# Delta rule on 32-column blocks, a rotation without products, and Strassen slots for the even layer's queries and keys

## The chip, the cores and the metric

The kernel runs on one core of one Trainium2 chip. All arithmetic is in 32-bit floats. The metric is the device time of one execution in microseconds (us), the median of several runs. The engines are named as in the profile: PE is TensorE (PEld its weight loads), DVE is VectorE, ACT is ScalarE, POOL is GpSimd, SP issues the DMAs. Each engine takes its instructions in the order in which they are written for it, and waits on semaphores that the others count up.

## The reference

Two networks of two layers each run one after the other on 512 latent tokens (and, in the first network, 256 context tokens) of width 1024. The change lies in the first layer of the first network, the "even" one. It projects the normed input to queries, keys and values of a differential attention (4 heads, each with two maps of 64 channels), and of a gated delta rule (4 heads of 128 channels, in both directions). What matters here:

```python
def apply_rope(x, cos, sin):
    xf = x.astype(f32).reshape(*x.shape[:-1], x.shape[-1] // 2, 2)
    x0, x1 = xf[..., 0], xf[..., 1]
    out = jnp.stack([x0 * cos - x1 * sin, x0 * sin + x1 * cos], axis=-1)
...
    decay = jnp.exp(jnp.where(causal, g[..., :, None] - g[..., None, :], -jnp.inf))
    kk = jnp.einsum('bhncd,bhnsd->bhncs', k, k)
    lmat = jnp.where(strict, beta[..., :, None] * decay * kk, 0.0)
    rhs = jnp.concatenate([beta[..., None] * v, (beta * jnp.exp(g))[..., None] * k], axis=-1)
    sol = lax.linalg.triangular_solve(jnp.eye(GDN_CHUNK, dtype=f32) + lmat, rhs,
                                      left_side=True, lower=True, unit_diagonal=True)
...
    def step(s, inp):
        u = u0_c - w_c @ s
        o = qg_c @ s + aqk_c @ u
        s = gl_c[..., None, None] * s + jnp.swapaxes(kg_c, -1, -2) @ u
```

## The kernel before, in words

Activations lie with channels on the 128 partitions and tokens along the row: T = 768 tokens (512 latent, 256 context), NT = 6 tiles of 128 tokens. KD = 8 blocks of 128 make up the width of 1024. Weights come through a ring of two buffers, WC[0] and WC[1], 256 output columns each (a slot). SP fills a buffer again when a semaphore says that its products are done. Every engine has one hand-written program; nothing plans the order at run time.

**The slots of even_qk.** Queries and keys of the differential attention are 1024 columns, four slots of two 128-column tiles. The first slot's tiles are begun by `first_tiles` (L1094) while the normed input appears. The other three slots are six plain products by `cols_phase` (L770): eight steps of 512 and 256 tokens each. `copies` on ACT (even tiles) and DVE (odd tiles) brings them to `F`. Each 32-bit product stands in the trace as two records, with a weight load each. Behind it come the gates (L1131) and the values (L1121). Other stages of the kernel (up0 is the first) already use slots by Strassen's scheme: DVE makes sums of weight blocks (`block_sums`) and of input blocks (`input_differences`, `input_sums`), PE makes seven products of half size instead of eight (L970), ACT copies two of them out of PSUM and DVE combines all seven (`combine`). Semaphores: u_ws and u_bs for the sums, u_m for the products, u_copy, u_free and u_out for the copies and combinations.

**The differential heads.** For each of four heads, queries and keys are scaled (L2917, d_norm), a product with the matrix rotA swaps neighbours of each pair of channels (L1222), and DVE multiplies by the tables sinA and cosA and adds (L2923 to L2925). Between these PE makes later column tiles of the layer (L770) and modulation rows (L1058); then scores, softmax, transposes and the product with the values follow. POOL meanwhile makes the short convolution of the delta heads before, four channel blocks a round (L3454 to L3462).

**The delta heads.** Each head has 12 matrices of 128 by 128, 6 tiles in 2 directions d. The unit triangular matrix (from gL, made of the key products psc and the gate gB) is inverted by doubling: level e joins blocks of width 2^e. The inverse Y stands in gY, its transpose X in gX. Level 0 is a masked copy of gL over an identity (L3006) and a transpose (L3009). For e = 1 to 5 PE makes L times Y in three groups of four tiles (`products`, L1361), ACT copies them to gS (L2146), PE multiplies by X (`updates`, L1377), and DVE copies the entries of the level under a mask into gY (L3029) and transposes (L3023). These products are 64x64, two a tile. The last level joins the two halves of 64 (`last_products` L1388, `last_updates` L1400). Then W is made (L1437), and a scan over the six tiles runs both directions step by step (L1451 to L1464), with DVE keeping the state.

In the gaps of the levels stands work for the next head n: on PE its sums of squares (`delta_sums`) and of decays (`delta_decay`), both L1195, on POOL its squares (L3494) and decay rows (L3503), on ACT its silus, logarithms and exponentials, on DVE `gates_of`, `differences`, `beta_gate` and `normalise`. The output of the head before (`head_out`) is also made there.

Of the kernel before, what the change touches and what calls it, by code (L numbers as in the profile page):

```python
# [17 lines left out]
P = 128  # L18
D = 1024
KD = D // P  # L20
LAT, CTX = 512, 256
# [16 lines left out]
R_CY, R_X, R_Y = 3 * (LAST - 1) + 2, 2 + 3 * (LAST - 2) + 2, 2 + 3 * (LAST - 1)  # L38
QUARTER = [(slice(0, 32), slice(32, 64)), (slice(96, 128), slice(64, 96))]
CORNER = [(slice(64, 128), slice(0, 64)), (slice(0, 64), slice(64, 128))]  # L40
QUARTERS = (slice(0, 64), slice(64, 128))
# [16 lines left out]
def shape_constants():  # L58
# [6 lines left out]

    r = np.zeros((P, P))
    e = np.arange(0, P, 2)
    r[e + 1, e] = -1.0
    r[e, e + 1] = 1.0
    c["rotA"] = r  # L70
# [14 lines left out]
    idx = (p % 64) // 2  # L85
    c["cosA"] = np.cos(ang)[:, idx].T
    c["sinA"] = np.sin(ang)[:, idx].T
    lev = []
    for b in range(LAST):
        w = 1 << b  # L90
        same = p[:, None] // (2 * w) == p[None, :] // (2 * w)
        low = same & (p[:, None] // w % 2 == 1) & (p[None, :] // w % 2 == 0)
        lev.append(np.stack([low.T, low], 1))
    c["levels"] = np.stack(lev, 1).reshape(P, LAST * 2 * P)
# [8 lines left out]
def offsets(parts):  # L103
    at, out = 0, {}
    for name, width in parts:
# [5 lines left out]
CONST_PARTS = [("ident", P), ("ones", P), ("sel32", 34), ("half", P), ("rotA", P), ("upto", 2 * P),  # L111
               ("near", GRID), ("dil", 2 * P), ("cosA", LAT), ("sinA", LAT),
               ("levels", LAST * 2 * P), ("invp", 1)]
# [16 lines left out]
LINEAR = [("even_qk", 2, 4), ("even_v", 1, 3), ("even_b", 4, 8),  # L130
# [10 lines left out]
STAGES = [("up0", 22), ("down0", (4, 4, 3)), ("up1", 22), ("down1", (4, 4, 3)), ("sc_in", 12), ("mup0", 16),  # L141
# [27 lines left out]
def views(nc, ctx):  # L169
# [11 lines left out]
    extra = sb("extra", 3 * P)  # L181
    psl = ctx.enter_context(nc.psum_tensor("ps_lin", [P, 2, 1024], F32))
# [20 lines left out]
    m["levels"] = cut(const, CONST_AT["levels"][0], LAST, 2, P).bitcast(mybir.dt.uint32)  # L203
# [37 lines left out]
    m["gL"], m["gX"], m["gY"] = (cut(h, i * 1536, 12, P) for i in range(3))  # L241
    m["gq"], m["gk"], m["gv"] = ([m["FB"][:, 4 * i, :]] + [cut(t, i * T, T) for t in (big, x, big)] for i in range(3))
# [31 lines left out]
    m["STR"] = {"up0": (up_sums, up_weights, up_parts),  # L274
# [117 lines left out]
def network(nc, a):  # L392
    with ExitStack() as ctx:
# [40 lines left out]
        def _(sp):  # L434
# [312 lines left out]
        def _(pe):  # L747
# [360 lines left out]
            cols_phase("even_qk", 2, T, begun_tiles=2)  # L1108
# [201 lines left out]
            def delta_head(h):  # L1310
# [30 lines left out]
                if h:  # L1341
                    pe.wait_ge(s.r_oln, h)
# [2307 lines left out]
```

## Time and profile before

| what | value |
|---|---|
| median of 3 runs | 3975.91 us |
| lowest, highest | 3975.55, 3978.28 us |
| profiled execution, its own time | 3969.4 us |
| span of its profile | 3966.6 us |
| PE busy | 3847.7 us, 97% |
| DVE, ACT, POOL busy | 55%, 21%, 18% |
| mean granted PE clock | 0.996 |

Start times in the rows count from the span's start. A row of the timeline merges neighbouring instructions of one line: its length reaches from the first start to the last end, "x" is their count, and the brackets hold idle time ahead of it and what ended it. Since a matmul's end lies behind the start of the next one, the spacing of starts tells more than the lengths.

### The profile page before, as it was taken

How to read it: one execution, taken by the hardware profiler on the slowest of the kernel's cores; microseconds unless marked ns; L12 is line 12 of the kernel's file. 1: busy time of each engine (PE TensorE's matmuls, PEld its weight loads, DVE VectorE, ACT ScalarE, POOL GpSimd, SP SyncE). 2: the span in 40 equal slices, each digit the busy share in tenths (PEclk: the TensorE clock that was granted, in tenths of full speed). 3: DMA queues.
4: the chain of work that ended last, by engine and by line, in shares of the span. 5: the costliest groups of instructions: out<-in, count | busy, mean ns of one | idle time of the engine just before them, and what ended most of it. 6: DMA issues, size and time to landing. Idle time of an engine off the chain costs nothing.

```text
span 3966.6 us, 48576 instructions
## 1 busy us (share of the span) xinstructions
PE 3847.7 (97%) x18642; PEld 2876.9 (73%) x18642; DVE 2168.3 (55%) x3779; ACT 824.2 (21%) x1463; POOL 712.9 (18%) x570
## 2 busy tenths in 40 slices
PE   7999978999999999999999999999999999999998
PEld 3445567565555555688888877888789898778886
DVE  2144476354446312326555665664788888556546
ACT  2144565221010014632110101000311111110002
POOL 0038853100000000000000001120144343121200
PEclk9999999999999999999999999999999999999999
DMA  5244300131211121112322322232222222122321
GB/s 182 85 162 167 117 23 2 65 96 53 63 53 59 58 74 33 42 53 76 85 85 94 83 79 85 85 107 90 77 70 69 63 74 69 53 85 85 101 85 64
DMA packets 381407, 312.19 MB, mean 79 GB/s; under 512 B 9552, under 2 KB 349904, under 8 KB 381136
## 3 DMA queue, kind: packets, MB, share of 16 engines
q1 hardware_dynamic: 381264, 310.23, 25.2%
q8 instruction: 97, 1.59, 0.2%
q14 instruction: 46, 0.38, 0.0%
HBM read 308.10 MB, written 2.10 MB: 78 GB/s over the span
## 4 chain that ended last, share of the span: by engine, by line
PE 92%; DVE 3%; ACT 3%; issue 1%; DMA 1%; SPq 0%; DVEq 0%; ACTq 0%
PE ps_lin L970 18%; PE ps_lin L870 10%; PE ps_d L970 9%; PE ps_lin L770 7%; PE ps_lin L1706 6%; PE ps_d L870 5%; PE ps_c L970 4%; PE ps_lin L753 4%; PE ps_lin L816 3%; PE ps_d L753 3%; PE ps_lin L1121 3%; PE ps_c L870 3%; PE ps_d L1495 2%; PE ps_c L753 2%; PE ps_d L1706 1%; PE ps_d L1058 1%
## 5 line engine op out<-in xcount | busy, mean ns | idle before, releaser
L3430 POOL TENSOR_TENSOR rstd<-square 128x512 f32<-128x512 f32 (+2 forms) x12 | 15.1, 1258 | 1556.1 <-ACT square L1893 1556.1
L970 PE MATMUL ps_lin<-arena,ring 128*128 128x256 f32 (+1 forms) x800 | 217.2, 424 | 1.1 <-DVE arena L2572 1.1
L870 PE MATMUL ps_lin<-arena,ring 128*128 128x256 f32 (+1 forms) x864 | 214.1, 401 | 0.0
L970 PEld LDWEIGHTS ps_lin<-arena,ring 128*128 128x128 f32 x800 | 151.9, 190 | 60.8 <-issue 2.9
L870 PEld LDWEIGHTS ps_lin<-arena,ring 128*128 128x128 f32 x864 | 164.2, 190 | 41.0
L970 PE MATMUL ps_lin<-hid_in,arena 128*128 128x256 f32 x832 | 188.6, 380 | 3.6 <-DVE arena L2599 3.6
L770 PE MATMUL ps_lin<-hid_in,ring 128*128 128x512 f32 (+1 forms) x576 | 189.3, 486 | 1.1 <-DMA ring<-in_even_w_in 1.1
L3433 POOL TENSOR_TENSOR rstd<-rstd,square 128x512 f32<-128x512 f32 (+2 forms) x58 | 75.2, 1297 | 630.6 <-ACT square L1893 629.6
L970 PE MATMUL ps_lin<-hid_in,mixed 128*128 128x384 f32 (+1 forms) x672 | 187.8, 433 | 0.0
L970 PE MATMUL ps_d<-arena,mixed 128*128 128x384 f32 (+1 forms) x672 | 187.8, 433 | 0.0
L2596 DVE TENSOR_TENSOR arena<-ring 128x1024 f32<-128x1024 f32 x84 | 103.1, 1227 | 147.6 <-PE ps_d L870 135.6
L970 PEld LDWEIGHTS ps_lin<-hid_in,arena 128*128 128x128 f32 x832 | 157.7, 190 | 27.6 <-DVE arena L2599 5.6
L770 PEld LDWEIGHTS ps_lin<-hid_in,ring 128*128 128x128 f32 x576 | 109.2, 190 | 79.4 <-issue 70.7
L970 PEld LDWEIGHTS ps_d<-arena,mixed 128*128 128x128 f32 x672 | 127.7, 190 | 53.1
L970 PEld LDWEIGHTS ps_lin<-hid_in,mixed 128*128 128x128 f32 x672 | 127.7, 190 | 53.1
L970 PE MATMUL ps_lin<-hid_in,ring 128*128 128x256 f32 x704 | 159.7, 380 | 3.4 <-issue 1.7
L970 PEld LDWEIGHTS ps_lin<-hid_in,ring 128*128 128x128 f32 x704 | 133.5, 190 | 23.7 <-issue 3.3
L2207 ACT ACTIVATE arena<-ps_lin 128x256 f32<-128x256 f32 (+1 forms) x96 | 39.0, 406 | 520.7 <-PE ps_lin L970 513.0
L2596 DVE TENSOR_TENSOR mixed<-ring 128x1024 f32<-128x1024 f32 (+1 forms) x66 | 80.6, 1222 | 116.1 <-PE ps_d L870 101.1
L1893 ACT ACTIVATE square<-resid 128x512 f32<-128x512 f32 (+2 forms) x104 | 63.2, 612 | 359.0 <-DVE resid L2746 99.3
L3569 POOL TENSOR_TENSOR arena<-ring 128x1024 f32<-128x1024 f32 x32 | 77.1, 2411 | 297.3 <-PE ps_d L1706 201.2
L1877 ACT ACTIVATE arena<-ps_lin 128x256 f32<-128x256 f32 (+1 forms) x32 | 13.1, 410 | 563.2 <-PE ps_lin L870 563.2
(545 smaller groups left out, 8100.1 us busy)
## 6 DMA issues: line engine op xcount, KB each, us to landing
ring<-in_ffn_w_in SPq DMA_DIRECT2D x88, 512.0 KB, 5.0
resid<-in_ada_w SPq DMA_DIRECT2D x20, 2048.0 KB, 8.1
ring<-in_mlp_w_up SPq DMA_DIRECT2D x64, 512.0 KB, 4.3
ring<-in_mlp_w_down SPq DMA_DIRECT2D x64, 512.0 KB, 4.4
ring<-in_attn_w_qkv SPq DMA_DIRECT2D x64, 512.0 KB, 4.5
ring<-in_ffn_w_out SPq DMA_DIRECT2D x32, 512.0 KB, 4.4
ring<-in_even_w_in SPq DMA_DIRECT2D x28, 512.0 KB, 5.1
ring<-in_sc_w_in SPq DMA_DIRECT2D x24, 512.0 KB, 4.6
```

Of the source, the lines that this page charges most:

```text
L753: last = mm(out, lhs, rhs, start=(j == 0), stop=(j == len(pairs) - 1))
L770: last = mm(psl[:, par, u:v], lhs, rhs[:, u:v], start=(j == 0), stop=(j == len(pairs) - 1))
L816: last = mm(psl[:, n, at:at + v - u], w[:, k, n * P:(n + 1) * P], O[:, k, u:v], start=(k == 0), stop=(k == KD - 1))
L870: last = mm(prod[i - 1], lhs[:, j, :], rhs(p), start=(g == j == 0), stop=(g == G - 1 and j == np_ - 1))
L970: last = mm(out, lhs[:, j, :], rhs[:, j, :], start=(j == 0), stop=(j == 3))
L1121: last = mm(psl[:, t % 2, 0:width], H[:, k, t * P:(t + 1) * P], weights[:, k, :], start=(k == 0), stop=(k == KD - 1))
L1495: last = mm(psd[:, u:v], WC[h % 2][:, k, P:2 * P], H[:, k, u:v], start=(k == 0), stop=(k == KD - 1))
L1706: last = mm(out, lhs[:, j, :], rhs[:, j, :], start=(j == 0), stop=(j == 3))
L1893: fn(SQ[:, k % 2, u:v], X[:, k, u:v], ACT.Square).then_inc(s.n_sq, 1)
L2596: tt(ws["sum"][:, 0:np_, :], r1, r2, add)
L3433: tt(acc, acc, m["SQ"][:, k % 2, c0:c1], ALU.add).then_inc(s.n_acc, 1)
L3569: tt(ws["sum"], r1, r2, ALU.add)
```

## The change

Three things change together.

1. **Levels up to the fifth keep 32-column blocks.** New tiles cX, cY and cS hold, for each of the 12 matrices, only the four diagonal blocks of 32 by 32, that is 128 partitions by 32 columns. `turned_blocks` brings gL in this form by products with an identity; levels e = 0 to 4 are masked copies and transposes of 6 tiles by 32 columns for each direction, and `products` and `updates` make four 32x32 products a tile, in two groups (one a direction) instead of three. Level 5, the pair step, joins neighbouring blocks of 32: `pair_products` and `pair_updates`. ACT and DVE then place the diagonal blocks and the pairs in gY and gX for the last level, which stays. gX and gY are cleared once by DVE; POOL sets the identity in cY for the next head.
2. **Work for the next head is re-ordered.** Its squares move from POOL to ACT. Its first sum stands behind the pair step, its second sum and its two decay sums between the steps of the scan; the logarithms, exponentials, `beta_gate`, `differences` and `normalise` move there as well. The transposes of the keys go to psc. A head's key products now wait for r_diff and r_qe of both directions.
3. **Rotation and even slots.** The host orders the query and key channels of each map so that the first parts of the pairs are 32 neighbours and the second parts the next 32. DVE then rotates by reading the other 32 partitions, without a product. The last three slots of even_qk use Strassen's scheme, with products in the order 3, 4, 5, 2, 1, 7, 6.

The core of the diff:

```diff
-LINEAR = [("even_qk", 2, 4), ("even_v", 1, 3), ("even_b", 4, 8),
+LINEAR = [("even_qk", 2, 1), ("even_v", 1, 3), ("even_b", 4, 8),
...
-            for sl in range(2):
-                sp.wait_ge(buf_full[1], BUFS["even_qk"] + sl + 1)
-                fill_cols(ew, sl, 512 + sl * 256)
+            sp.wait_ge(buf_full[1], BUFS["even_qk"] + 1)
+            fill_cols(ew, 0, 512)
+            sp.wait_ge(s.u_m, 3)
+            fill_cols(ew, 1, 768)
...
-                half_done("even_qk")(sl)
+                sp.wait_ge(s.u_m, 7 * (sl + 1) + 3)
...
             pe.wait_ge(s.wg_in, 16)
+            pe.wait_ge(s.u_out, 6)
...
-                for j, (q, ps) in enumerate([("QN", psc[:, 0:LAT]), ("KN", psc[:, LAT:2 * LAT])]):
-                    pe.wait_ge(s.d_norm, 2 * h + j + 1)
-                    mm(ps, m["rotA"], m[q][:, 0:LAT], start=True, stop=True).then_inc(s.d_rot, 1)
+                pe.wait_ge(s.d_rs, 2 * h + 2)
...
                 pe.wait_ge(s.r_norm, 2 * h + 2)
+                pe.wait_ge(s.r_diff, 2 * h + 2)
+                pe.wait_ge(s.r_qe, 2 * h + 2)
...
+                def products(e, d):
+                    c = 2 * (e - 1) + d
+                    pe.wait_ge(s.r_y, R_Y * h + c + 1)
+                    if e == 1:
+                        pe.wait_ge(s.r_vt_out, h + 1)
+                    for t in range(NT):
+                        j = d * NT + t
+                        for r in QUARTERS:
+                            last = mm(CYB[d][r, t * 32:(t + 1) * 32], gL[r, j, r], cY[r, j, :], start=True, stop=True)
+                    last.then_inc(s.r_cy, 1)
+
+                def updates(e, d):
+                    c = 2 * (e - 1) + d
+                    pe.wait_ge(s.r_cy_out, R_CY * h + c + 1)
+                    pe.wait_ge(s.r_x, R_X * h + c + 1)
+                    for t in range(NT):
+                        j = d * NT + t
+                        for r in QUARTERS:
+                            last = mm(YCYB[d][r, t * 32:(t + 1) * 32], cX[r, j, :], cS[r, j, :], start=True, stop=True)
+                    last.then_inc(s.r_ycy, 1)
...
+                pair_products()
+                pair_updates()
+                if n is not None:
+                    pe.wait_ge(s.r_kq_out, 2 * h + 2)
+                    if h == 0:
+                        pe.wait_ge(s.mod_new, H_EVEN)
+                    delta_sums(n, 0, SIDE)
...
+                    if i == 0:
+                        pe.wait_ge(s.r_ln, 2 * n + 1)
+                        delta_sums(n, 1, SIDE)
+                    if i == 2:
+                        pe.wait_ge(s.r_ln, 2 * n + 2)
+                        delta_decay(n, 0, SIDE)
+                    if i == 4:
+                        pe.wait_ge(s.r_qe, 2 * n + 1)
+                        delta_decay(n, 1, SIDE)
```

On ACT and DVE of a delta head (heads of the levels and of the scan):

```diff
+                for e in range(1, PAIR):
+                    for d in range(2):
+                        act.wait_ge(s.r_cy, R_CY * h + 2 * (e - 1) + d + 1)
+                        fn(half(cS, d), blocks(CYB[d]), ACT.Copy).then_inc(s.r_cy_out, 1)
+                    if e == 1 and h:
+                        out_rstd(h - 1)
+                    if n is not None and e > 1:
+                        silu(n, e - 2)
+                        if e < 4:
+                            head_square(n, e - 2)
...
+                if n is not None:
+                    gate_of(h)
+                    logs()
+                    log_of(n, 0, SIDE)
+                else:
+                    gate_of(h)
...
+                    if i == 1:
+                        log_of(n, 1, SIDE)
+                        exp_gate(n)
+                    if i == 2:
+                        rstd_of_head(n)
+                    if i == 3:
+                        exp_rows(n, 0, SIDE)
+                        exp_decay(n, 0)
+                if n is not None:
+                    exp_rows(n, 1, SIDE)
+                    exp_decay(n, 1)
...
+                for e in range(PAIR):
+                    for d in range(2):
+                        dve.wait_ge(s.r_eye, 2 * h + 4)
+                        dve.wait_ge(s.r_ycy, R_YCY * h + 2 * e + d + 1)
+                        dve.copy_predicated(half(cY, d), over_tiles(m["levels"][:, e, d, :]), blocks(YCYB[d]))\
+                            .then_inc(s.r_y, 1)
+                        dve.wait_ge(s.r_y, R_Y * h + 2 * e + d + 1)
+                        dve.transpose(half(cX, d), half(cY, d)).then_inc(s.r_x, 1)
+                    if e == 0 and n is not None:
+                        gates_of(n)
+                    if e == 1:
+                        query_key(0)
+                        query_key(1)
...
+                    if e == 2 and h:
+                        head_out(h - 1, 0)
+                    if e == 3 and h:
+                        head_out(h - 1, 1)
...
+                    if i == 2:
+                        beta_gate(n)
+                        differences(n, 0, SIDE)
+                    if i == 3:
+                        normalise(n, 0)
+                    if i == 4:
+                        normalise(n, 1)
+                if n is not None:
+                    differences(n, 1, SIDE)
```

Here PAIR is 5, QUARTERS are the four slices of 32 partitions, h is the head and n the next one (none for the last).

## Rows read from the trace of the kernel before

**Rows 1.** The page: busy us of PE (share of span, instructions); chain that ended last

```profile
PE 3847.7 (97%) x18642; PEld 2876.9 (73%) x18642; DVE 2168.3 (55%) x3779; ACT 824.2 (21%) x1463; POOL 712.9 (18%) x570
...
PE 92%; DVE 3%; ACT 3%; issue 1%; DMA 1%; SPq 0%; DVEq 0%; ACTq 0%
```

**Rows 2.** Timeline, PE, rest of even_qk: start us, us, engine, line, operation

```profile
61.47 62.08 PE L770 MATMUL ps_lin<-hid_in,ring 128*128 128x512 f32 x192
```

**Rows 3.** Timeline, PE, two neighbouring Strassen slots of the up0 stage

```profile
858.19 5.32 PE L970 MATMUL ps_lin<-arena,ring 128*128 128x384 f32 x16
...
876.25 5.32 PE L970 MATMUL ps_lin<-arena,ring 128*128 128x384 f32 x16
```

**Rows 4.** Timeline, DVE: last operation before even_qk; four input sums of up0

```profile
53.63 0.22 DVE L2827 TENSOR_REDUCE small<-arena 128x1 f32<-128x64 f32 x1
...
828.36 1.96 DVE L2554 TENSOR_TENSOR arena<-hid_in 128x384 f32<-128x384 f32 x4
```

**Rows 5.** Timeline, PE: the rotation of the first differential head

```profile
187.10 1.98 PE L1222 MATMUL ps_c<-mixed,const 128*128 128x512 f32 x4
...
188.92 10.48 PE L770 MATMUL ps_lin<-hid_in,ring 128*128 128x512 f32 x32
```

**Rows 6.** Timeline, POOL: start of the last round of convolutions

```profile
419.29 1.44 POOL L3439 COPY mixed<-arena 128x768 f32 x1 [2.87 <-DVE mixed L2917]
```

**Rows 7.** Timeline, PE: delta heads, from the first to the stage behind them

```profile
498.31 1.60 PE L1321 MATMUL ps_c<-arena 128*128 128x128 f32 x12
...
559.68 1.50 PE L1321 MATMUL ps_c<-arena 128*128 128x128 f32 x12
...
566.35 0.68 PE L1361 MATMUL ps_lin<-hid_in 64*64 64x64 f32 x16
...
575.02 1.56 PE L1195 MATMUL ps_d<-square,const 128*128 128x512 f32 x4
...
594.77 1.61 PE L1377 MATMUL ps_lin<-arena,hid_in 64*64 64x64 f32 x32 [1.72 <-issue]
...
597.67 2.16 PE L1195 MATMUL ps_d<-resid,const 128*128 128x512 f32 x4
...
599.76 1.43 PE L1388 MATMUL ps_lin<-hid_in 64*64 64x64 f32 x24
...
605.57 0.39 PE L1451 MATMUL ps_c<-arena,hid_in 128*128 128x128 f32 x2
...
682.54 1.50 PE L1321 MATMUL ps_c<-arena 128*128 128x128 f32 x12
...
732.99 2.82 PE L794 MATMUL ps_lin<-mixed,ring 128*128 128x512 f32 x8 [1.19 <-DVE arena L3071]
```

**Rows 8.** Timeline, ACT and DVE: single operations of the second delta head

```profile
561.72 1.28 ACT L1829 ACT_TABLE_LOAD   x1
...
563.01 0.81 ACT L2132 ACTIVATE arena<-ps_lin 128x768 f32<-128x768 f32 x1
...
568.97 0.60 ACT L2146 ACTIVATE arena<-ps_lin 128x512 f32<-128x512 f32 x1 [0.25 <-PE ps_lin L1361]
...
562.28 1.03 DVE L3006 COPY_PREDICATED hid_in<-const,hid_in 128x768 f32<-128x768 uint32 x1
...
571.03 0.73 DVE L3029 COPY_PREDICATED hid_in<-const,ps_lin 128x512 f32<-128x512 uint32 x1 [0.26 <-PE ps_lin L1377]
...
537.71 0.77 DVE L3042 STREAM_TRANSPOSE hid_in<-hid_in 32x192 f32<-32x192 f32 x2
```

**Rows 9.** Timeline, PE: four small products (eight records) with 32 weight columns

```profile
511.98 0.28 PE L1065 MATMUL ps_d<-mixed,const 128*32 128x40 f32 x8
```

**Rows 10.** Groups, PE, 0 to 745 us, shapes apart: count, busy us, mean ns

```profile
L1065 PE MATMUL ps_d<-mixed,const 128*32 128x40 f32 x32 | 1.1, 216 | 0.0
```

**Rows 11.** Windows: busy us of PE, PEld, DVE, ACT, POOL; granted clock

```profile
592.00:594.00 2.00, 0.68 (x16) 0.57 (x16) 1.98 (x2) 1.31 (x3) 2.00 (x2) 1.00 0.00 0
...
596.00:598.00 2.00, 1.77 (x25) 1.49 (x22) 1.38 (x3) 0.00 (x0) 1.23 (x1) 0.50 0.04 8
```

More of the change, by code:

```diff
@@ new lines, in delta_head @@
+                for d in range(2):
+                    turned_blocks(d)
+                for t in range(NT):
+                    last = pe.transpose(psc[:, t * P:(t + 1) * P], gk[:, t * P:(t + 1) * P], ident)
+                last.then_inc(s.r_kt, 1)
+                for e in range(1, PAIR):
+                    for d in range(2):
+                        products(e, d)
+                    if e == 1:
+                        if h:
+                            pe.wait_ge(s.r_oln, h)
+                        for t in range(NT):
+                            c = slice(t * P, (t + 1) * P)
+                            last = mm(psd[:, c], gk[:, c], gq[:, c], start=True, stop=True)
+                        last.then_inc(s.r_kq, 1)
+                    for d in range(2):
+                        updates(e, d)
+                    if e == 2 and h == 0:
+                        mod_slot(H_EVEN - 1, MOD_STEPS)
@@ L1817, in _ @@
             chain = Chain(act, s.act_step)
-            def copies(name, iters, dst, width):
-                b = BUFS[name]
-                with act.Fori(0, iters) as i:
-                    for sl in range(2):
-                        act.wait_ge(buf_full[0], b + 2 * i + sl + 1)
-                        fn(flat(dst)[:, ds((4 * i + 2 * sl) * width, width)], psl[:, 0, 0:width], ACT.Copy)\
-                            .then_inc(buf_free[0], 1)
             def logs():
@@ L1933, in _ @@
             shifts("mix0", T)
-            copies("even_qk", 2, m["F"], T)
+            act.wait_ge(buf_full[0], BUFS["even_qk"] + 1)
+            fn(m["F"][:, 0, :], psl[:, 0, 0:T], ACT.Copy).then_inc(buf_free[0], 1)
+            for u in range(3):
+                if u:
+                    act.wait_ge(s.u_free, 3 * u - 1)
+                for i in range(2):
+                    act.wait_ge(s.u_m, made(u, 3 + i))
+                    fn(m["STR"]["even_qk"][2][i], m["PROD"][2 + i][:, 0:T // 2], ACT.Copy).then_inc(s.u_copy, 1)
             act.wait_ge(s.g_raw, 1)
@@ new lines, in delta_head @@
+                for q in QUARTERS[1:]:
+                    diagonal(q)
+                act.wait_ge(s.r_ycy, R_YCY * (h + 1) - 2)
+                for d in range(2):
+                    pair(d, 0)
+                for d in range(2):
+                    lo, up = CORNER[d]
+                    act.wait_ge(s.r_cy, R_CY * (h + 1) - 1 + d)
+                    fn(half(gS, d)[up, :, lo], corners(CYB[1][up, :]), ACT.Copy).then_inc(s.r_cy_out, 1)
+                act.wait_ge(s.r_x, R_X * (h + 1))
+                for d in range(2):
+                    pair(d, 1)
```

426 lines of the change are left out of this document (196 added, 230 removed).

## Prediction

> **What bounds the kernel now.** I read the page first: PE is busy 97% of the span and carries 92% of the chain that ended last [rows 1]. So time is won only where PE has less to do or waits less. The timeline of PE then shows three stretches that the change touches. The rest of even_qk is one unbroken block of 62.08 us [rows 2]. The four differential heads are dense too; in each the rotation takes PE from 187.10 to 188.92 [rows 5]. The delta heads are the only long stretch with idle between PE's groups: the first takes 61.37 us, the two after it 61.43 each, the last, up to the 1.19 us of waiting ahead of even_out, 49.26 [rows 7]. There a level is a circle of PE product, ACT copy, PE product, DVE masked copy, so it is bound by latencies and by the order in the queues of ACT and DVE. Five levels of a middle head, with four sums for the next head among them (1.5 us each), last from 566.35 to 599.76, which is 33.4 us [rows 7].
>
> **Part 1: even slots.** Six plain products go; three Strassen slots come. Two such slots of the same width start 18.06 us apart [rows 3], so PE needs 3 x 18.06 = 54.2 us for the 62.0 us that the block takes up to the next stage. DVE must first make the sums. It is free at 53.85 [rows 4]. Four sums of 384 columns take 1.96 us, the next starts 0.47 behind the last [rows 4]: 20 input sums make 9.4 us, and the weight sums, 2560 columns in four operations, 3.0. DVE ends at 66.3, then it copies tile 1 (0.9 us), which frees the bank for the third product at 67.2. PE is there at 61.47 + 5.16 = 66.6, so it waits 0.6. At the end PE must wait for DVE's last combination, a 384-column addition of 0.5 us and two hand-overs: 0.85. Sum: 54.2 + 0.6 + 0.85 - 62.0 = **-6.3 us**. On SP the fills of the last two slots and of the values wait for counts of Strassen products, each at least four products (10 us) ahead of its use; that cover hides their landing, and without it one late fill would cost up to its own length, which I leave to the range.
>
> **Part 2: rotation.** PE loses two products a head: 188.92 - 187.10 = 1.82 us, four times **-7.3 us** [rows 5]. DVE gets eight operations on 32 partitions instead of two on 128, some 5 us more a head. They lie under the two later tiles (10.5 us each, the second starts at 188.92 [rows 5]) and the scores that need them wait for both tiles anyway, so I price them at nothing. Cover is thin elsewhere: POOL idled only 2.87 us ahead of its last round of convolutions [rows 6], and a head on PE gets 1.8 us shorter. About 1 us of slack is left for what eight DVE operations from SBUF may slow POOL by. POOL's end is needed only at the first delta head's levels; I take 0, and up to 3 us as the upper bound.
>
> **Part 3: delta heads.** First the unit. A group of products was 16 pairs of load and product on 64x64 tiles; it is now 24 products, 48 pairs, on 32x32. No row shows this shape. The nearest burst is eight records with 32 weight columns: 0.28 us together [rows 9], of which one alone is 0.216 [rows 10], so they start 9 ns apart, each with its load. The nearest sustained row is a 64x64 group: 16 in 0.68 us [rows 7], 31 ns a pair once the same latency is taken off, and there two parts of the array share the work. I take 9 ns, since the new products use four separate parts and the burst used four too: 0.43 us a group plus 0.22 latency. The other end, 31 ns, is 1.5 us a group.
>
> The other steps of a level are now 192 columns wide. ACT: 0.60 us for 512 and 0.81 for 768 give 0.34. DVE masked copy: 0.73 and 1.03 give 0.36. Transpose: 0.77 / 2 = 0.38 or a little less [rows 8]. Both directions follow each other on each engine. The first direction's product is done at 0.65 and ACT's copy at 1.03; PE issues the second direction's product until 1.21 (it can begin only at 0.78, when DVE has transposed and copied for it); the update is done at 1.86, the masked copy at 2.26, and with hand-overs of 0.05 to 0.1 the next level begins at 2.35. Four levels are left.
>
> Middle head, from its first product to the next head's:
> - Start. The key products now also wait for the decay of the next head, whose differences DVE makes only behind the scan: 1.15 us to finish the scan, 2.05 for the differences, 0.9 for ACT's exponentials. PE stands idle 4.3 us. Then key products, gL, sums for the head before, turned blocks, and the level-0 copies: the first level starts 9.75 us in, where it was 6.67 (566.35 - 559.68 [rows 7]), although level 0 itself is cheaper.
> - Levels: the first 2.35 + 1.35 for the query products on PE; the second 2.35 + 0.9, what two query-key operations on DVE take beyond their cover; the third 2.35 + 0.85, from a silu, a square and a table load of 1.28 [rows 8] in ACT's queue; the fourth 3.0 to its last masked copy, + 3.1 because ACT's second silu waits for the head output that DVE makes behind its level, and behind it in ACT's queue stands the copy that PE needs. Sum 16.25, for 33.4.
> - Pair step, corner and W, counted from the last masked copy: pair products, copy and updates to 1.85; ACT's diagonal and pair copies to 3.2 (the next head's sum on PE lies under them); corner products to 3.9, their copy to 4.4, updates to 5.3, the last copies to 6.3. W's products take 2.75, to 9.05. Corner and W took 5.8 before (605.57 - 599.76 [rows 7]). Then ACT is late: gate 0.85, table load 1.28, logarithm 1.05 hold it to 9.9, its two copies of W end at 11.5, and the scan runs from 12.5.
> - Scan: 13.6 us as before (605.57 to the next head at 621.1 [rows 7], less 1.9 of lead-in), three sums of 1.45 moved into it, and 1.75 where moved work holds ACT or DVE: 0.55 for the table load ahead of exp_gate, 0.35 for DVE's differences ahead of a state, 0.85 for ACT's wait on them. Sum 19.7, so 32.2 from the last masked copy.
>
> Together 9.75 + 16.25 + 32.2 = 58.2, against 61.43: -3.2 each, -6.4 for two.
>
> First head: it needs no start wait; two memsets (2.5 us) stand ahead of level 0, and neither the head output nor its stall exists: 6.9 + 14.0 + 32.2 = 53.1 against 61.37, -8.3. Last head: no silu and no moved work, but the start wait: 9.75 + 12.4 + 25.0 = 47.2 against 49.26, -2.1. Together **-16.8 us**. The moved sums, squares and decay rows themselves cost what they did; they only change place. POOL's decay rows come later, still some 15 us ahead of the scan that needs them.
>
> **Part 4: the clock.** Between 592 and 594 PE was busy 0.68 us of 2, and behind that stretch the granted clock was 0.50, that is 1.2 instead of 2.4 GHz [rows 11]. There 32 records took 1.61 us, where two groups of 16 need 1.15, and a sum took 2.16 where 1.56 is usual [rows 7]; with the group between them I put such a drop at 1.4 us. The new heads have three kinds of gap as long: the start (3 times), the stall in the third level (2) and the late scan start (3). Eight drops for two that vanish: 6 x 1.4 = **+8.4 us**.
>
> Total: -6.3 - 7.3 - 16.8 + 8.4 = -22.0 us. The profiled execution took 3969.4 us (span 3966.6), 6.5 under the median of the three shown; it becomes 3947.4, and the median 3975.9 becomes 3953.9.
>
> **Rivals.** (a) The small products don't come at 9 ns. At the sustained 31 ns a group takes 1.05 us more; PE becomes the bound in the levels: +2.5 to +3.4 us each, turned and pair groups +2 each, about +15 a head, +60 in all: 3953.9 + 60 = 4014. 60 us over 22 ns is 2.7 us for each ns a pair, so it decides from about 17 ns a pair. For it: 48 pairs a group is three times the instructions and no sustained row is under 15 ns an instruction [rows 7]. Against it: the burst [rows 9]. The Trainium skill, TensorE: Matmul & The Clock Gate, section "Wait — 56ns, not 53.3ns?", says that starts of matmuls never come closer than about 25 ns however small they are. By that rule the sum would be about +21 us instead of -22, by that same slope. The trace disagrees for the burst on separate tiles, and no run here shows a long row of them. (b) The delta part gives nothing because the moved work and the clock take all: only parts 1 and 2 remain, -13.6, 3962. For it: three waits that I found by following the queues are each of 2 to 4 us, and one more per head is enough. (c) The clock doesn't fall in the new gaps, or the gaps are covered: -30.4, 3945.5. (d) POOL becomes the bound of the differential heads: part 2 gives 4 instead of 7, 3957; this lies inside the forecast.
>
> **Numbers.** Chances: the forecast 0.48, (a) 0.15, (b) 0.15, (c) 0.15, (d) 0.07. The time is 3953.9. The forecast's own range is 3938 to 3962. For 8 in 10 I take 3935 to 3970, which holds (b), (c) and (d) and leaves (a) out. A difference under 0.2%, 8 us, can't be told from none. Faster: the forecast, (c) and (d) but for 0.02, and 0.11 of (b), so 0.79. Same: 0.08. Slower: 0.13.
>
> **What the new profile would show.** Part 1: PE's even_qk in three slots 18.06 us apart and a gap near 0.6 in the first. Part 2: no rotation, and heads of 78.7 us instead of 80.5. Part 3: level period near 2.4 us with gaps in PE; 48 pairs in about 0.45 us of issue. If a group takes over 0.8 us, (a) is at work. The start gap of 4 us and the ACT work ahead of W's copies should be visible as waits of PE on ACT, and the granted clock should be 0.5 behind them. The prediction is wrong if PE's groups are slow, if POOL's rounds leave no idle and PE waits for convolutions, or if the scan loses more than 2 us a head to ACT.

## The result, and the profile after

The changed kernel takes 3984.37 us (median of 19 runs, 3978.50 to 3993.28), the kernel before 3975.97 (19 runs, 3970.35 to 3982.40). The ratio is 1.0022, with a 95% interval of 1.0015 to 1.0029: slower by 8.4 us, just over what can be told from no change. The prediction was 3953.9, in a range of 3935 to 3970. It was wrong in size and in sign.

The page of the changed kernel, busy time, instruction DMA and the chain that ended last, answers to [rows 1]:

```profile
PE 3831.3 (96%) x20570; PEld 2865.6 (72%) x20570; DVE 2173.9 (55%) x3830; ACT 821.8 (21%) x1480; POOL 700.9 (18%) x564
...
q8 instruction: 112, 1.84, 0.2%
...
PE 91%; DVE 3%; ACT 3%; issue 2%; DMA 1%; SPq 0%; DVEq 0%; ACTq 0%
```

PE is busy 16.4 us less than before, and the span is 13.2 us longer (3979.8 for 3966.6). The spans differ by more than the 8.4 us of the medians because the profiled execution before was 6.5 us under its median, the one after 2.8 (3981.6). PE has 1928 more product records (and as many more weight loads), and "issue", time in which the engine waited for nothing that the profile shows, has gone from 1% to 2% of the chain. So the loss is neither more busy time of PE nor a larger share of waits on a named engine. Where it lies is seen by cutting the span at the borders of the stages. This is the timeline of PE where even_qk runs, and the first product of the delta heads:

```profile
61.47 5.32 PE L1126 MATMUL ps_lin<-arena,ring 128*128 128x384 f32 x16
67.31 5.40 PE L1126 MATMUL ps_lin<-hid_in,mixed 128*128 128x384 f32 x16 [0.51 <-DVE arena L2922]
...
80.28 5.32 PE L1126 MATMUL ps_lin<-arena,ring 128*128 128x384 f32 x16
...
98.34 5.32 PE L1126 MATMUL ps_lin<-arena,ring 128*128 128x384 f32 x16
...
117.31 2.79 PE L1175 MATMUL ps_d<-hid_in,arena 128*32 128x512 f32 x32 [0.74 <-DVE arena L2790]
...
485.19 1.60 PE L1365 MATMUL ps_c<-arena 128*128 128x128 f32 x12
```

Part 1 came as predicted: slots 18.06 us apart, a wait of 0.51 (0.6 predicted), the next stage at 117.31 instead of 123.5: -6.2. The delta heads start at 485.19, for 498.31 [rows 7]: -13.1 for parts 1 and 2 up to there, -13.6 predicted. Then the delta heads take 259.05 us, up to the 1.18 us of waiting ahead of even_out at 745.42, where they took 233.49 [rows 7]: +25.6, against -8.4 predicted (-16.8 for part 3, +8.4 for the clock). All that follows is 0.8 us longer. The loss is the delta heads. PE's timeline of the second one, for the levels two to five and the pair step:

```profile
551.84 2.90 PE L1365 MATMUL ps_c<-arena 128*128 128x128 f32 x12 [4.19 <-ACT resid L2086]
...
558.49 1.11 PE L1398 MATMUL ps_lin<-inverse,hid_in 32*32 32x32 f32 x96
559.53 1.60 PE L1464 MATMUL ps_d<-arena 128*128 128x128 f32 x12
561.06 0.60 PE L1408 MATMUL ps_lin<-inverse 32*32 32x32 f32 x47
561.92 0.74 PE L1408 MATMUL ps_lin<-inverse 32*32 32x32 f32 x49 [0.25 <-issue]
562.63 1.12 PE L1398 MATMUL ps_lin<-inverse,hid_in 32*32 32x32 f32 x79
565.48 0.47 PE L1398 MATMUL ps_lin<-inverse,hid_in 32*32 32x32 f32 x17 [1.72 <-issue]
565.71 1.52 PE L1408 MATMUL ps_lin<-inverse 32*32 32x32 f32 x96
567.12 0.43 PE L1398 MATMUL ps_lin<-inverse,hid_in 32*32 32x32 f32 x14
568.92 1.38 PE L1398 MATMUL ps_lin<-inverse,hid_in 32*32 32x32 f32 x82 [1.36 <-issue]
570.08 0.85 PE L1408 MATMUL ps_lin<-inverse 32*32 32x32 f32 x45
572.48 0.99 PE L1408 MATMUL ps_lin<-inverse 32*32 32x32 f32 x51 [1.55 <-issue]
573.35 1.31 PE L1398 MATMUL ps_lin<-inverse,hid_in 32*32 32x32 f32 x77
576.04 0.53 PE L1398 MATMUL ps_lin<-inverse,hid_in 32*32 32x32 f32 x19 [1.38 <-issue]
577.33 1.50 PE L1408 MATMUL ps_lin<-inverse 32*32 32x32 f32 x96 [0.77 <-ACT inverse L2215]
579.43 1.06 PE L1417 MATMUL ps_lin<-inverse,hid_in 32*32 32x32 f32 x48 [0.59 <-DVE inverse L3118]
```

The gaps stand inside groups: a group of 96 products needs nothing new behind its 79th, its 14th or its 45th, and yet PE stops there for 1.4 to 1.7 us. Between two long gaps lie always nearly the same number of products: 17 + 96 + 14 = 127, then 82 + 45 = 127, then 51 + 77 = 128. Counted with the weight loads and the few waits that have a record of their own, the stretch from the end of one such gap to the start of the next holds exactly 256 instructions of PE, 16 times in the four heads. The same in the first head, and below it the strip of DMA traffic from 500 to 516 us, 40 slices of 0.4 us, in GB/s:

```profile
501.33 0.56 PE L1408 MATMUL ps_lin<-inverse 32*32 32x32 f32 x41 [1.59 <-issue]
501.82 0.28 PE L1068 MATMUL ps_d<-mixed,const 128*32 128x40 f32 x8
502.03 0.87 PE L1398 MATMUL ps_lin<-inverse,hid_in 32*32 32x32 f32 x79
505.30 0.47 PE L1398 MATMUL ps_lin<-inverse,hid_in 32*32 32x32 f32 x17 [2.40 <-issue]
```

```profile
GB/s 0 0 0 0 0 0 41 0 0 0 0 0 0 0 0 0 41 0 0 0 0 20 0 0 0 41 0 0 0 0 0 0 0 0 0 41 0 0 0 0
```

41 + 8 + 79 = 128 again. The peaks of 41 are packets of 16 KB of the instruction queue q8, at 502.7, 506.5, 510.2 and 514.2 (the 20 is a packet of 8 KB of another queue, q14). In the DMA records of the trace the first three end at 503.98, 507.48, 511.12; PE goes on at 505.30, 508.73 and 512.56, always 1.25 to 1.45 us behind. So PE in the levels runs at the pace at which instructions arrive: from one long gap's end to the next it takes 3.3 to 4.1 us, mean 3.7, for 256, some 14 ns each. A level is 384 instructions, so some 5.6 us, where the prediction had 2.35. The sixteenth stretch, in the last head, takes 6.4 us: the next packet starts only 4.1 us after PE has gone on, why no run shows, and PE stands 3.59 us inside the pair step:

```profile
716.42 0.75 PE L1417 MATMUL ps_lin<-inverse,hid_in 32*32 32x32 f32 x38 [3.59 <-issue]
```

The windows of the second head's levels and of what follows them (busy us of PE, PEld, DVE, ACT, POOL; granted clock) answer to [rows 11]:

```profile
558.49:579.43 20.94, 13.26 (x782) 11.89 (x781) 10.37 (x24) 10.68 (x18) 14.61 (x11) 0.66 0.02 5
579.43:612.41 32.98, 29.55 (x296) 24.10 (x296) 13.87 (x36) 18.56 (x40) 2.83 (x3) 0.91 0.01 2
```

No engine is busy for more than 0.7 of the levels (20.94 us). The granted clock of the whole delta part is 0.80, where it was 0.99.

### The profile page after: what moved, and what is told of

Its sections match the earlier page's. It is cut to its first block, busy times and chain, and to the rows that moved or that the text cites. A ratio compares the mean times of both kernels' runs of the same rounds, so it can differ in the third digit from the quotient of the medians.

```text
span 3979.8 us, 52443 instructions
## 1 busy us (share of the span) xinstructions
PE 3831.3 (96%) x20570; PEld 2865.6 (72%) x20570; DVE 2173.9 (55%) x3830; ACT 821.8 (21%) x1480; POOL 700.9 (18%) x564
## 4 chain that ended last, share of the span: by engine, by line
PE 91%; DVE 3%; ACT 3%; issue 2%; DMA 1%; SPq 0%; DVEq 0%; ACTq 0%
PE ps_lin L973 18%; PE ps_lin L873 10%; PE ps_d L973 9%; PE ps_lin L1769 6%; PE ps_lin L773 6%; PE ps_d L873 5%; PE ps_c L973 4%; PE ps_lin L756 4%; PE ps_lin L819 3%; PE ps_d L756 3%; PE ps_lin L1164 3%; PE ps_c L873 3%; PE ps_d L1558 2%; PE ps_c L756 2%; PE ps_d L1769 1%
## 5 line engine op out<-in xcount | busy, mean ns | idle before, releaser
L973 PEld LDWEIGHTS ps_lin<-hid_in,ring 128*128 128x128 f32 x704 | 133.4, 190 | 23.8 <-issue 3.3
L1935 ACT ACTIVATE arena<-ps_lin 128x256 f32<-128x256 f32 (+1 forms) x32 | 13.2, 412 | 563.9 <-PE ps_lin L873 563.9
L773 PE MATMUL ps_lin<-hid_in,ring 128*128 128x256 f32 (+1 forms) x384 | 127.6, 488 | 1.0 <-DMA ring<-in_even_w_in 1.0
L873 PE MATMUL ps_lin<-arena 128*128 128x256 f32 x512 | 115.7, 379 | 0.0
```

What stands on the lines that cost most here:

```text
L773: last = mm(psl[:, par, u:v], lhs, rhs[:, u:v], start=(j == 0), stop=(j == len(pairs) - 1))
L873: last = mm(prod[i - 1], lhs[:, j, :], rhs(p), start=(g == j == 0), stop=(g == G - 1 and j == np_ - 1))
L973: last = mm(out, lhs[:, j, :], rhs[:, j, :], start=(j == 0), stop=(j == 3))
```

## The experiments

Times are medians; ratios are to runs of the kernel before on the same chip (3974.3 to 3976.1 us), with the 95% interval.

**1. Old delta heads, with the even slots and the rotation (the prediction's parts 1 and 2) kept.** The levels, the pair step, the order of the side work and the constants for them are those of the kernel before.

> The kernel before with the Strassen slots of even_qk and the rotation on DVE, its delta heads untouched. If the whole loss is in the delta heads, as the two traces suggest (first delta head starts at 485.2 instead of 498.3), this runs at 3976 - 13 = 3963 us, ratio to before 0.9967. Rival, the new even slots and the rotation cost something further down (a later fill, a clock drop): 3968 or more.

3962.65 us, ratio 0.9964 (0.9950 to 0.9977). Parts 1 and 2 are worth 13 us, and the delta heads cost 22. It beats both kernels.

**2. Key products first.**

```diff
                 pe.wait_ge(s.r_norm, 2 * h + 2)
-                pe.wait_ge(s.r_diff, 2 * h + 2)
-                pe.wait_ge(s.r_qe, 2 * h + 2)
...
                 last.then_inc(s.r_kk, 1)
+                pe.wait_ge(s.r_diff, 2 * h + 2)
+                pe.wait_ge(s.r_qe, 2 * h + 2)
```

> The changed kernel, but PE's key products stand ahead of the two waits on the next head's decay again. Theory A (the start gap of 4.2 us is a chain scan, DVE differences, ACT exponentials, PE, DVE): the products hide in it, and gL's second half is ready some 2 us earlier in each of three heads: 3984 - 6 = 3978 us, up to 3 less if the clock stays up as well. Rival, the levels are limited by the supply of instructions and take back what the start gives: no change, 3984.

3978.36 us, ratio 1.0009 (1.0000 to 1.0018): 6 us better than the changed kernel, as expected. The start gap was real and is paid.

**3 and 4. Half the products, or half their columns.** Both leave the inverse incomplete: the first has no products for the rows 64 to 127, the second none for half of the columns of each block.

```diff
-                        for r in QUARTERS:
+                        for r in QUARTERS[0:2]:
```
```diff
-  mm(CYB[d][r, t * 32:(t + 1) * 32], gL[r, j, r], cY[r, j, :], ...)
+  mm(CYB[d][r, t * 32:t * 32 + 16], gL[r, j, r], cY[r, j, 0:16], ...)
```

> The changed kernel, with the products of levels two to five for the first two of the four 32-row blocks only (the inverse is left incomplete): 192 instead of 384 load and product instructions a level, each as before. Theory A (instructions come in packets of 256, one every 3.6 us, and PE stands still between them): a level falls from about 5.2 us to 2.4 to 3.0, the gaps marked issue vanish inside groups, 16 levels give about 40 us: 3944. Rival, the level is bound by its latencies and by ACT's and DVE's queues: a level loses only the 0.5 us a group of shorter issue, 4984 groups apart, some 15 us: 3969.

> The changed kernel, with the same number of products in levels two to five, each with 16 moving columns instead of 32 (the inverse is left incomplete). Theory A (supply of instructions): no change within 5 us of 3984, the gaps marked issue of 1.3 to 2.6 us stay, one for every 128 products. Rival, the array's time for each product: a group is shorter by up to half, 20 us or more in all: 3964.

Half the count: 3953.88 us (two runs), ratio 0.9942 (0.9924 to 0.9960), between theory and rival and nearer to the theory. Half the columns: 3983.96, ratio 1.0021 (1.0011 to 1.0031), no change. The groups of PE between 480 and 745 us for the two lines of products and updates (count, busy us, mean ns, idle before and its releasers), first of the changed kernel, then with half the count, then with half the columns:

```profile
L1398 PE MATMUL ps_lin<-inverse,hid_in 32*32 32x32 f32 x1536 | 24.5, 215 | 20.4 <-issue 18.5 <-DVE inverse L3118 1.5
L1408 PE MATMUL ps_lin<-inverse 32*32 32x32 f32 x1536 | 24.5, 223 | 12.3 <-issue 11.2 <-ACT inverse L2215 1.1
```

```profile
L1408 PE MATMUL ps_lin<-inverse 32*32 32x32 f32 x768 | 20.2, 214 | 6.4 <-ACT inverse L2215 6.2
L1398 PE MATMUL ps_lin<-inverse,hid_in 32*32 32x32 f32 x768 | 20.1, 210 | 7.2 <-DVE inverse L3118 6.3
```

```profile
L1398 PE MATMUL ps_lin<-inverse,hid_in 32*32 32x16 f32 x1536 | 24.5, 200 | 20.7 <-issue 18.9 <-DVE inverse L3118 1.5
L1408 PE MATMUL ps_lin<-inverse 32*32 32x16 f32 x1536 | 24.4, 202 | 11.0 <-issue 9.8 <-ACT inverse L2215 1.1
```

The 29.7 us of "issue" stay with half the columns (28.7) and are gone with half the count; what is left is the idle of a circle bound by ACT and DVE. Together with the equal count between the gaps and the packets that end ahead of each restart, this puts the loss on the number of instructions, not on the columns that the array streams. Of the 30.5 us, 19.1 are idle of the two lines (32.7 to 13.6) and 8.7 their own busy time (49.0 to 40.3), which falls too when each group has half the products. The clock was as low with half the count (0.81), so the 30.5 us are not the clock's. One wait that the supply had hidden comes out in its second head, that of ACT's silu:

```profile
565.21 1.49 PE L1408 MATMUL ps_lin<-inverse 32*32 32x32 f32 x48 [2.61 <-ACT inverse L2215]
```

**5. Side work in another order.**

```diff
 # ACT
+                gate_of(h)
+                logs()            # behind the last silu, not ahead of W's copies
 # DVE
                     if e == 2 and h:
                         head_out(h - 1, 0)
-                    if e == 3 and h:
                         head_out(h - 1, 1)
 # PE
+                    if e == 3: delta_sums(n, 0, SIDE)      # was behind pair_updates()
...
+                delta_sums(n, 1, SIDE)                     # was behind step 0 of the scan
```

> The changed kernel with its side work in another order: the head output of the head before behind level two on DVE (both parts), ACT's gate and the table load for the logarithms behind the last silu instead of ahead of W's copies, the next head's first sum on PE inside the levels (behind the updates of level three of five), its second one between W's products and the scan instead of in the scan. If the PE gap of 1.58 us ahead of the scan is ACT's gate and table load, as the queue shows, it falls under 0.9, the sum in the levels lies under the supply of instructions at no cost, and one sum of 1.3 us leaves the scan: three heads by 1.0 + 1.4 + 0.8 us, 3984 - 10 = 3974 us. Rival: the table load now delays the diagonal copies on ACT by as much as it freed: no change, 3984.

3983.28 us, ratio 1.0019 (1.0010 to 1.0028): 1.1 us better at most, the rival. PE's timeline of its second head, the sum in the levels and the corner:

```profile
575.15 2.93 PE L1239 MATMUL ps_d<-square,const 128*128 128x512 f32 x4
578.01 1.08 PE L1398 MATMUL ps_lin<-inverse,hid_in 32*32 32x32 f32 x96
...
585.01 2.34 PE L1437 MATMUL ps_lin<-hid_in 64*64 64x64 f32 x23 [1.36 <-ACT hid_in L2231]
...
589.50 4.02 PE L1488 MATMUL ps_lin<-hid_in,arena 128*128 128x128 f32 x24
```

The sum is free in the levels: from the updates ahead of it to the pair step it takes 9.1 us with the sum (571.84 to 580.93) and 9.35 without it (570.08 to 579.43), and the 96 products behind it run without a gap, since instructions arrive while the sum runs. But the corner now waits 1.36 us for ACT's copies, and the half clock falls on the corner and on W (4.02 us instead of 2.92).

**6. One idle product a level.**

```diff
                     for d in range(2):
                         updates(e, d)
+                    pe.wait_ge(s.r_kt_out, h + 1)
+                    mm(psc[:, 0:512], ones, m["cosA"][:, 0:512], start=True, stop=True)
```

> The changed kernel with one product more behind the updates of each of the levels two to five, 128 rows by 512 columns of a constant, whose result nobody reads (16 in all, some 0.86 us each). Theory A (the low granted clock is paid outside the levels too: key products, sums, corner and W at half speed, some 5 us a head) and the product lies in the time in which PE waits for instructions anyway: the clock stays at 1.0, 3984 - 12 = 3972 us. Rival: the product is added to a path that the supply doesn't cover: 16 x 0.86 = 14 us more, 3998.

3986.41 us, ratio 1.0021 (1.0012 to 1.0030). Neither: the granted clock of the delta part rose only from 0.80 to 0.84, and of the 16 added products (1.1 us each at full clock, 2.1 at half, so some 18 us in all or more) all but some 2 us lay under waits that were there anyway. It shows how much time the levels have to give away, and leaves the price of the clock open.

**7. Products on 64x64 tiles.** POOL copies the diagonal 32x32 blocks of L into the otherwise empty buffer gX; a product then takes two rows of blocks at once. Of the edit, PE's part, shortened:

```diff
+                    if e == 2: pe.wait_ge(s.d_norm, ...)       # POOL's copy is made
...
-                        for r in QUARTERS:
-                            mm(CYB[d][r, ...], gL[r, j, r], cY[r, j, :], ...)
+                        for r in (QUARTERS if e == 1 else (slice(0, 64), slice(64, 128))):
+                            mm(CYB[d][r, ...], (gL if e == 1 else gX)[r, j, r], cY[r, j, :], ...)
```

> The changed kernel with the products of levels three to five (not the updates) made on 64x64 tiles from a copy of L that holds only its 32x32 diagonal blocks (four copies and two memsets on POOL a head): two products a tile instead of four, so 288 instead of 384 load and product instructions in each of these levels. Theory A (supply of instructions, 3.6 us a packet of 256): 12 such levels by 1.3 us: 3984 - 14 = 3970 us, and fewer gaps marked issue. Rival: POOL's new work is late for the third level, or holds up the operands of the scan: 3984 or more.

3974.05 us, ratio 0.9995 (0.9986 to 1.0004): 10.3 us better. Its groups:

```profile
L1400 PE MATMUL ps_lin<-inverse,hid_in 64*64 64x32 f32 (+1 forms) x960 | 34.6, 239 | 7.1 <-issue 3.7 <-POOL hid_in L3623 1.7 <-DVE inverse L3121 1.5
L1411 PE MATMUL ps_lin<-inverse 32*32 32x32 f32 x1536 | 22.4, 220 | 7.4 <-issue 4.2 <-ACT inverse L2218 3.2
```

1152 instructions fewer (12 levels by 96) took the "issue" of the two lines from 29.7 to 7.9 us. Their idle of every kind fell by 18.2 (32.7 to 14.5), since other waits came out, and their busy time rose by 8.0, because 48 products on 64x64 tiles take longer than 96 on 32x32 (2.77 us for 1.50 at half clock). That is why 22 us less of "issue" gave only 10.

**8 to 12. Put together.** Eight is two, five and seven. Nine has the 64x64 products in all four levels, the key products first and the head output early. Ten adds five, but leaves the first sum where it was. Eleven is ten with the first level of the first head on 32x32 tiles. Twelve is eleven with another start of a head: values turned right behind the key products, output sums behind the turned blocks.

> The changed kernel with the key products first, the side work in the other order and the 64x64 products together. If the three are independent: 3984 - 6 - 10 - 14 = 3954 us, under the kernel before and under the version with the old delta heads (3962.7). If they share the same slack, the supply of instructions has hidden part of it: 3965 or more, and the old delta heads stay the better ones.

3967.09 us, ratio 0.9978 (0.9969 to 0.9987). The number is the rival's, its reason is not: what the three gave one by one (6.0, 1.1 and 10.3 us) adds up to 17.4, and 3984.4 - 17.4 = 3967.0. So the three came out as independent; the expected sum missed because it took 10 and 14 for five and seven, which gave less.

> The changed kernel with the key products first, the products of all four levels on 64x64 tiles, and the head output behind level two on DVE, so that ACT's silu in level four no longer waits for it. The sums and the table loads stay where the change put them. Theory A: 3984.4 - 6 (key products) - 10.3 (64x64 in three levels) - 3 (the fourth level) - 3 (ACT's wait of 1.46 us in two heads) = 3962 us. Rival: the first level isn't bound by the supply, because instructions fetched ahead cover it, and the silu's wait is hidden behind something else: 3968.

3971.72 us, ratio 0.9993 (0.9984 to 1.0002): worse than theory and rival. PE's first level of the first head shows why; POOL, late with its convolutions, had not copied L:

```profile
498.76 2.78 PE L1400 MATMUL ps_lin<-inverse,hid_in 64*64 64x32 f32 x48 [8.22 <-POOL hid_in L3622]
```

> The same, and ACT's gate and table load behind the last silu, the second sum between W's products and the scan (the first sum stays behind the pair step). Theory A: the gap of 1.58 us ahead of the scan goes in three heads and the sum covers W's copies: 3962 - 5 = 3957 us. Rival, what the run with the other order of side work showed: the 2.1 us of ACT work moves onto the diagonal copies, PE waits for them 1.4 us instead, and the low clock falls on the corner and on W: 3962 or more.

3967.59 us, ratio 0.9983 (0.9974 to 0.9992), with the same wait (7.99 us), so it does not decide between its theory and its rival.

> The version before (64x64 products, key products first, gate and table load behind the last silu, second sum ahead of the scan), but the first level of the first head on 32x32 tiles again, because PE waited 8.2 us there for POOL's masked copy of L. Theory: the two runs on 64x64 tiles missed their expectation by this one wait: 3967.6 - 6 = 3961.5 us. Rival: the instructions that were fetched ahead during that wait run out sooner, and the later levels of the head give it back: 3966.

3962.55 us, ratio 0.9975 (0.9964 to 0.9985): near the theory. Removing the one wait gave 3 to 5 us (by the ratios, and by the medians). The 32-column heads now are about as good as the old ones in experiment 1 (3962.65, ratio 0.9964; the intervals overlap), not better.

> The same, and at the start of a head PE turns the values right behind the key products and makes the output sums of the head before only behind the turned blocks; both waits on the next head's decay stand there too. The trace has the turned blocks behind a wait of 2.69 us, 1.5 us of turning and up to 2.9 us of sums, while L was ready before: three heads by 3 to 4 us, so 3961.5 - 10 = 3951 us. Rival: L itself (POOL's product with the decay, then DVE) sets the start, and ACT's late output logarithm delays its copy of the keys, so that the levels start as late as before: 3960.

3965.66 us, ratio 0.9981 (0.9972 to 0.9990): the rival's mechanism, and 3 us worse than eleven. POOL and DVE make the second half of L at the same time as in eleven (DVE's operation starts at 549.35, there at 549.40), and PE's sum of 2.93 us now stands behind it, so the levels of the second head start at 555.08 instead of 553.31:

```profile
550.37 0.87 PE L1382 MATMUL ps_lin<-const,hid_in 32*32 32x32 f32 x48 [2.76 <-DVE hid_in L3103]
551.16 2.93 PE L1239 MATMUL ps_d<-square,const 128*128 128x512 f32 x4
```

**13 and 14. The even slots alone, the rotation alone**, each on the kernel before. Experiment 1 had shown something not asked for: ACT waited 5.94 us for POOL's last convolution in the first delta head.

> The kernel before with only the Strassen slots of even_qk. Theory (the rotation on DVE slows POOL, the slots don't): PE is 6.2 us shorter, POOL's rounds of convolutions start as much earlier and keep their pauses of 3.05 and 2.87 us: 3976 - 6 = 3970 us, ratio 0.9984. Rival, POOL is the bound with anything ahead of it shortened: 3974 or more.

> The kernel before with only the rotation on DVE. Theory (POOL bound in the differential heads): PE loses 7.3 us of products, but POOL has only 5.9 us of pauses to give and its operations get some 6 us longer beside DVE's new ones, so the last convolution ends no earlier and ACT waits for it in the first delta head: 3976 - 2 = 3974 us. Rival, POOL's wait lies under something else in most runs: 3976 - 7 = 3969 us, as in the two parts together (3962.7).

Slots alone: 3969.71 us, ratio 0.9980 (0.9971 to 0.9989), -6.4. Rotation alone: 3971.43, ratio 0.9986 (0.9977 to 0.9995), -4.6, between the theory and its rival. Together they gave 13.0 in experiment 1, alone 11.0 in sum; the intervals are too wide to tell these apart. POOL's last round of convolutions, with the slots alone and with the rotation alone, against [rows 6], and ACT's waits for its end, with the rotation alone and in the changed kernel:

```profile
414.43 1.44 POOL L3488 COPY mixed<-arena 128x768 f32 x1 [2.81 <-DVE mixed L2966]
```

```profile
419.66 1.35 POOL L3435 COPY mixed<-arena 128x768 f32 x1 [0.58 <-POOL arena L3458]
...
504.09 1.09 ACT L2138 ACTIVATE arena<-ps_lin 128x512 f32<-128x512 f32 x2 [5.96 <-POOL arena L3458]
```

```profile
495.36 0.55 ACT L2215 ACTIVATE inverse<-ps_lin 128x192 f32<-128x192 f32 x2 [3.72 <-POOL arena L3565]
```

With the slots POOL keeps its pause; with the rotation the pause is gone and POOL sets the time of the differential heads. Its 12 convolutions are busy 204 us before and 211 after the change, the same operations; with the slots alone they are busy 204, with the rotation alone 211. So it is DVE's new operations that slow them.

## Why the prediction was wrong, step by step

- **Part 1, -6.3:** right, -6.2 in the trace, -6.4 measured alone.
- **Part 2, -7.3, POOL priced at 0:** PE's side was right (the delta heads start 13.1 us earlier for both parts). POOL's was not. It ends its convolutions only 6.0 us earlier, and in the changed kernel ACT waits 3.72 us for it in the first head. That is rival (d), given 0.07 (part 2 gives 4 instead of 7); alone the rotation gives 4.6, so POOL costs 2.7, inside the 3 us that the prediction allowed as the upper bound.
- **Part 3, the unit:** right. A group of 96 products (two groups of the prediction, one a direction) takes 1.04 to 1.11 us at full clock; less 0.22 of latency and over 95 steps that is 9 ns each, the 9 ns taken from [rows 9]. At half clock it takes 1.50 us, some 13 ns each. Rival (a), in which the small products are slower, is wrong as a mechanism, and so is the rule of the Trainium skill weighed there (TensorE: Matmul & The Clock Gate, "Wait — 56ns, not 53.3ns?", no starts closer than about 25 ns): these start 9 ns apart in the mean of a whole group.
- **Part 3, "the next level begins at 2.35": this is the step that failed.** It let PE issue at 9 ns for as long as it liked and had no term for bringing the instructions. The runs showed in its place a supply of one packet of 256 instructions in 3.7 us, so 5.6 us for the 384 of a level. The four stretches of levels took 21.8, 20.9, 23.2 and 21.0 us, 86.9 in all, where the sum had 14.0, 16.25 twice and 12.4, 58.9: +28.0, of which up to 3.7 in the first head are POOL's (part 2). Experiment 3 takes 30.5 us away by half the count, experiment 4 nothing by half the columns, experiment 7 ten by a smaller cut. With half the count the four stretches take 15.7, 16.4, 16.4 and 13.6 us, 62.1 in all, near the 58.9 of the sum: its other terms for the levels were about right. The prediction had the fact in hand, "three times the instructions", and read it as a price per product. A sustained 3.7 us for 128 pairs is 29 ns a pair, by chance near rival (a)'s 31; the time stayed far under its 4014, because the supply binds almost only in the levels, and the waits that the prediction had counted there lie under it.
- **Where the stall goes:** the 3.1 us for ACT's silu, which the sum puts into the fourth level (part 4 of the prediction says the third), is hidden in the changed kernel by the supply (0.77 us of PE waiting for ACT at 577.33) and comes out at 2.61 where half the count is left out (experiment 3).
- **Starts:** 39.9 us for four, 36.2 predicted; the gap of 4.3 is 4.19. The key products behind it run at half clock in three heads (2.90 us for 1.50), 4.2 us that the prediction had under part 4.
- **Pair step to the end of the scan, with the clock:** 132.2 us for four, 121.6 + 8.4 predicted. The last head has the miss: the gap of 3.59 us inside its pair products, which is the supply again, and the corner and W at half clock.
- **Part 4, the clock:** right that it falls, too small in size. 1.4 us for a drop was for stretches of 3.4 us. From the levels on it now stays at half (1.2 GHz) for 17.1, 20.5, 20.5 and 30.7 us, one stretch a head; the mean over the levels of the second head is 0.66. PE was busy 13.26 of 20.94 us there; in the kernel before, at clock 1.00, it was busy 15.58 of 21 (571 to 592). Key products took 2.90 for 1.50, a sum 2.93 for 1.46, W in the last head 5.21 for 2.92. What it costs in all is not settled. As an estimate, the rows of the products at half clock outside the small ones (key and query products, sums, corner, W) add up to some 15 us more than at full clock; which of them lay under other waits no run separates.

By spans: +28.0 levels, +3.7 starts, +2.2 from the pair step to the end of the scan (with all 8.4 of the clock counted there), +0.5 ahead of the delta heads and +0.8 behind them make the 35.2 us between the predicted span, 3966.6 - 22.0, and 3979.8.

## What to carry to other kernels

Count instructions, not only time: where a stage issues loads and products closer than the 14 ns apart that were supplied here, and for more than the one or two packets of 256 that were ahead, ask what brings them, and look in the profile for "issue" gaps inside a group and for an equal count between them. Large products between the small ones were then nearly free (experiments 5 and 6). It follows, though no run tried it alone, that taking side work out of such a stage gives its cover away. A moved operation on DVE must be priced on POOL too, when POOL has only 3 us of pause a round.

## What the runs showed of the hardware

- Instructions come in packets of 16 KB for 256 of them. Once PE has caught up, a packet takes 0.9 to 1.3 us, PE goes on 1.2 to 1.6 us after its end, and the next packet starts some 1.1 to 1.7 us after that (once 4.1). From the last long gap of a head to the first of the next, PE executes 1536, 1280 and 1280 instructions, again whole packets. In the slow scan a packet starts only when some 100 to 290 of the instructions that had arrived are left, so there were never more than about two packets ahead (477 instructions at 609.59, late in the second head's scan, by this count), and PE stands still again in the first or second level of every head. The Trainium skill, Runtime: NRT & Kernel Launch, section Instruction fetch mechanics, tells of blocks of 256 and a queue of the sequencer's own, which the trace bears out, and that fetching is hidden because instructions are dispatched more slowly; here 29.7 us in two lines of one stage were not.
- A group of 96 products with half the columns (32x16) takes 1.08 us, the same as with 32x32.
- POOL's operations get longer beside eight 32-partition operations of DVE: the 48 products of a tap go from a mean of 1543 to 1582 ns, the 12 copies of five weights from 190 to 343.
